# The first expert's weight loads without a wait, and the tile tables in two halves among the first units' low parts

## The chip, the cores and the metric

The kernel runs on one core of a Trainium2 chip. The metric is the device time of one execution in microseconds (us); lower is better. The times shown are medians of several executions.

## The reference, cut to what matters

Two transformer blocks over 2048 tokens of width 1024. The part around the change is the mixture of experts of the first block: every token goes to 4 of 32 experts, each with a gate-and-up product of 1024 x 2048, a clamped SwiGLU and a down product of 1024 x 1024.

```python
def moe(hn, router_w, router_b, w_gu, b_gu, w_down, b_down):
    ...
    top_vals, top_idx = lax.top_k(logits, TOP_K)
    gates = jax.nn.softmax(top_vals, axis=-1)
    flat_e = top_idx.reshape(-1)
    order = jnp.argsort(flat_e)
    sorted_e = flat_e[order]
    tok = order // TOP_K
    xs = xt[tok]
    group_sizes = jnp.bincount(flat_e, length=N_EXPERTS).astype(jnp.int32)
    gu = lax.ragged_dot(xs, w_gu, group_sizes) + b_gu[sorted_e]
    gate = jnp.minimum(gu[:, ::2], SWIGLU_LIMIT)
    up = jnp.clip(gu[:, 1::2], -SWIGLU_LIMIT, SWIGLU_LIMIT)
    act = (up + 1.0) * (gate * jax.nn.sigmoid(SWIGLU_ALPHA * gate))
    y = lax.ragged_dot(act.astype(w_down.dtype), w_down, group_sizes) + b_down[sorted_e]
    ...
```

## The kernel before

The kernel runs in phases, one after another with a barrier between them: a mixer phase with the router (it writes, for each expert, a list of its tokens to HBM, `tok_list`, and leaves on chip the order in which experts are taken, `order`, and a count per expert, `n_mid`), the expert phase, a combine phase, and the phases of the second block. The change lies in the first 50 us of the expert phase (`expert_phase`, from L981), which starts at about 963 us in the trace.

**Weights.** An expert's weights come in 25 units (`UNITS`): four chunks of 512 columns of the gate-and-up matrix, four units each (units 0 to 15), then nine for the down matrix. A unit of the usual size is 128 x 1024 words, 512 KB. SyncE (SP) loads a unit from HBM into one of five slots of `stage` (L1077), ScalarE (ACT) copies it to the rounded high part `w_hi` (`high`, L1151), and VectorE (DVE) subtracts to make the low part `w_lo` (`low`, L1282), which counts up `lo_done`. Load m waits until low part m-5 is made, since both use one slot. So the loads, high parts and low parts of a unit follow one another, five units in flight at most.

**Tokens.** For a tile of 128 tokens GpSimd (POOL) reads the token numbers from the list by two small DMAs (`ids`, L1106), and then gathers the rows by an indirect DMA (`rows`, L1112). TensorE (PE) transposes the rows (L1502). ACT makes the high part of the transposed tile and a bf16 copy (`x_high`, L1162 and L1164), DVE the low part (`x_low`, L1287). Only then can TensorE run the tile's products: for each chunk 16 products with the high weights (L968, L969) and 8 with the low ones (L971).

**What sets the order.** Each engine's instructions stand in an order written by hand, and an engine never takes a later one while it waits in an earlier one. At the start of the phase:

- SP reads the first expert's number, waits for the token numbers of the first tile (`ids_in`, line 1080), and then issues loads 0 to 4, and each later one as `lo_done` allows.
- ACT issues five DMAs for the biases (L1140, L1145), then `high` of units 0 and 1, then `x_high` of tile 0, then `high` of units 2 to 15. In the tile (`first`) follow `high` 16, 17, and so on.
- DVE makes the tile tables (`tables`, L1382 to L1409): `n_mid` sorted into the experts' order, and the running sums `starts` and `rows64`; then it signals `tables_ready`. Then `low` 0 and 1, `x_low`, `low` 2 to 13. In the tile follow `low` 14 to 16, and then `gates` of chunk 0 (L1306 to L1312), which adds the bias and frees the accumulator for chunk 3.
- PE transposes tile 0, then waits before chunk c of a new expert's first tile for `lo_done` of unit 4c+3, before chunk 0 also for `x_ready` (both parts of the tile), and before chunk 3 for `gates` of chunk 0, since chunk 3 uses the accumulator of chunk 0.
- All engines but SP wait for `tables_ready` after their part of tile 0, in `experts`, since the loop over the second and later tiles takes its bounds from the tables. POOL's part of tile 0 is its gather alone.

Of the kernel before, what the change touches and what calls it, by code (L numbers as in the profile page):

```python
# [8 lines left out]
F32 = mybir.dt.float32  # L9
I32 = mybir.dt.int32  # L10
U32 = mybir.dt.uint32
ALU = mybir.AluOpType
ACT = mybir.ActivationFunctionType
AX = mybir.AxisListType.X
# [24 lines left out]
E, TOPK, CAP = 32, 4, SEQ  # L39
# [912 lines left out]
GU_CHUNKS = 2 * FF // BANK  # L952
# [22 lines left out]
def gate_rows(w_lo):  # L975


    return w_lo[:, 0:GU_CHUNKS, :, :].rearrange("p c k n -> p (c k n)").bitcast(F32).rearrange("p (k n) -> p k n", n=D)


def expert_phase(nc, I, S):  # L981
# [6 lines left out]
    with ExitStack() as ctx:  # L988
# [5 lines left out]
        w_lo = S["w_lo_gate"]  # L994
# [9 lines left out]
        pre = sb("pre", [P, BANK])  # L1004
# [16 lines left out]
        s = {n: sem(n) for n in names}  # L1021
# [11 lines left out]
        def read(eng, table, i, most):  # L1033
            return eng.value_load(S[table][0:1, bass.ds(i, 1)], min_val=0, max_val=most)
# [27 lines left out]
        def place(m):  # L1062

            c, k0, k1 = UNITS[m]
            return c, slice(k0, k1), stage[:, m % STAGES, 0:k1 - k0, :]
# [5 lines left out]
        @block.sync  # L1071
        def _(sp):
            def load(m, e):
                c, ks, staged = place(m)
                name, col = ("expert_w_gate_up", c) if c < GU_CHUNKS else ("expert_w_down", c - GU_CHUNKS)
                w = I[name][0, bass.ds(e, 1), ks.start * P:ks.stop * P, col * BANK:(col + 1) * BANK].squeeze(0)
                sp.dma_start(staged, w.rearrange("(k p) n -> p k n", p=P)).then_inc(st_in[m % STAGES], 16)  # L1077

            e = read(sp, "order", 0, E - 1)
            sp.wait_ge(s["ids_in"], 32)  # L1080
            for m in range(N_UNITS):
                if m >= STAGES:
                    sp.wait_ge(s["lo_done"], m - STAGES + 1)
                load(m, e)
            with sp.Fori(1, E) as i:
                e = read(sp, "order", i, E - 1)
                for m in range(N_UNITS):
                    sp.wait_ge(s["lo_done"], i * N_UNITS + (m - STAGES + 1))
                    load(m, e)
            for k in range(KD):  # L1090
                if k % 2 == 0:
                    sp.wait_ge(s["low_free"], k // 2 + 1)
                sp.dma_start(gate_rows(S["w_lo_gate"])[:, k, :], I["ple_gate_w"][0, k * P:(k + 1) * P, :]).then_inc(S[f"gate_in{k}"], 16)
# [179 lines left out]
        def _(dve):  # L1273
# [4 lines left out]
            def low(e, m):  # L1278

                c, ks, staged = place(m)  # L1280
                dve.wait_ge(s["hi_done"], e * N_UNITS + (m + 1))
                dve.tensor_tensor(w_lo[:, c, ks, :], staged, w_hi[:, c, ks, :], ALU.subtract).then_inc(s["lo_done"], 1)  # L1282

            def x_low(g):

                dve.wait_ge(s["x_hi_ready"], g + 1)
                dve.tensor_tensor(x_lo[:, :, :], TX[:, :].rearrange("p (k c) -> p k c", c=P), x_hi[:, :, :],  # L1287
                                  ALU.subtract).then_inc(s["x_ready"], 1)
# [87 lines left out]
            row_of_e = lambda ap: ap.unsqueeze(1).to_broadcast([P, E, E])  # L1376
            row_of_i = lambda ap: ap.unsqueeze(2).to_broadcast([P, E, E])
            flat = stage[:, :, :, :].rearrange("p b k n -> p (b k n)")
            tc = Chain(dve, s["table_chain"])

            def numbers(iota, zero):
                tc.link(dve.memset(iota, 1.0))  # L1382
                tc.link(dve.memset(zero, 0.0))
                tc.link(dve.tensor_tensor_scan(iota, iota, zero, 0.0, ALU.add, ALU.add))
                tc.link(dve.tensor_scalar(iota, iota, -1.0, None, ALU.add))

            def tables():


                part = lambda n: w_lo[:, GU_CHUNKS + n // 2, n % 2 * 4:n % 2 * 4 + 4, :].bitcast(F32).rearrange("p k (i e) -> p (k i) e", e=E)  # L1390
                sel, picked = part(0), part(1)
                iota, zero, order, n_mid, sorted_mid, cnt_t, ends_t, cnt, ends = (pre[:, n * E:(n + 1) * E] for n in range(9))
                numbers(iota, zero)
                tc.link(dve.tensor_copy(order, S["order"][:, :]))
                tc.link(dve.tensor_copy(n_mid, S["n_mid"][:, :]))
                tc.link(dve.tensor_tensor(sel, row_of_e(iota), row_of_i(order), ALU.is_equal))
                tc.link(dve.tensor_tensor(picked, sel, row_of_e(n_mid), ALU.mult))
                tc.link(dve.tensor_reduce(sorted_mid, picked, AX, ALU.add))
                tc.link(dve.tensor_scalar(sorted_mid[:, 0:1], sorted_mid[:, 0:1], 1.0, None, ALU.max))
                tc.link(dve.tensor_scalar(sorted_mid[:, E - 1:E], sorted_mid[:, E - 1:E], 1.0, None, ALU.max))  # L1400
                dve.tensor_copy(S["n_mid"][:, :], sorted_mid)
                tc.link(dve.tensor_scalar(cnt_t, sorted_mid, 2.0, None, ALU.add))
                tc.link(dve.tensor_scalar(cnt, sorted_mid, 4.0, None, ALU.add))
                tc.link(dve.tensor_tensor_scan(ends_t, cnt_t, zero, 0.0, ALU.add, ALU.add))
                tc.link(dve.tensor_tensor_scan(ends, cnt, zero, 0.0, ALU.add, ALU.add))
                tc.link(dve.memset(S["starts"][:, 0:1], 0))
                tc.link(dve.memset(S["rows64"][:, 0:1], 0))
                tc.link(dve.tensor_copy(S["starts"][:, 1:E + 1], ends_t))
                tc.link(dve.tensor_copy(S["rows64"][:, 1:E + 1], ends))  # L1409
                dve.sem_inc(s["tables_ready"], 1)  # L1410

            sel, picked = (flat[:, n * E * E:(n + 1) * E * E].rearrange("p (i e) -> p i e", e=E) for n in range(2))
            which = flat[:, 2 * E * E:2 * E * E + TILES * TOPK * E].rearrange("p (n e) -> p n e", e=E)
            e_of, row_f = (flat[:, 4096 + n * TILES * TOPK:4096 + (n + 1) * TILES * TOPK] for n in range(2))
            to_row, iota, zero, order, begin = (flat[:, 4096 + (4 + n) * E:4096 + (5 + n) * E] for n in range(5))
# [26 lines left out]
            def last(e, g, n):  # L1442
# [42 lines left out]
                low(n, 13)  # L1485
                take_y(e, g)

            tables()
            for m in range(2):
                low(0, m)  # L1490
            x_low(0)
            for m in range(2, 14):
                low(0, m)
            experts(dve, first, mid, last)

# [1940 lines left out]
```

## Time and profile before

| what | value |
|---|---|
| median of 3 runs | 5496.25 us |
| lowest and highest of them | 5495.29 and 5498.11 us |
| the profiled execution: first to last instruction (its own time is not listed apart from that) | 5506.9 us |
| TensorE busy | 5150.5 us, 94% |
| VectorE busy | 3222.5 us, 59% |
| ScalarE busy | 2175.2 us, 39% |
| GpSimd busy | 628.4 us, 11% |
| expert phase, first DMA issue to the last gather issued | 964 to about 3486 us |

Times in the trace are microseconds from the first instruction. "Idle before" in a row of the timeline is how long that engine did nothing before the row, and the arrow names what ended the wait. Engines with a q at the end (SPq, ACTq) are the queue's side of an engine: what they did is issue a DMA. A row with "x5" merges five instructions of one kind, and its second number runs from the first's start to the last's end. PE is TensorE's matmul, PEld its weight load.

### The profile page before, as it was taken

The page shows a single profiled execution, that of the slowest core. Times are in us where ns is not written, and L with a number is a line of the kernel's source. Part 1 is how long each engine was busy: PE and PEld are TensorE (multiplying, and loading weights), DVE is VectorE, ACT ScalarE, POOL GpSimd, SP SyncE. Part 2 cuts the span into 40 slices and gives each one's busy share as a digit, 9 for nine tenths or more (in the row PEclk, how much of TensorE's full clock was granted, in tenths as well). Part 3 has the DMA queues.
Part 4 walks back from the last instruction along what each step waited for, and adds up shares of the span by engine and source line. Part 5 has one row for each costly group of instructions (what it writes and reads, how often), then busy time and mean ns, then how long its engine had stood idle before and what let it go on. Part 6 is the DMA issues. An engine that isn't in the chain of part 4 may idle for free. (4 is left out here: it accounts for less than half of the span.)

```text
span 5506.9 us, 77588 instructions
## 1 busy us (share of the span) xinstructions
PE 5150.5 (94%) x25057; PEld 3525.0 (64%) x25454; DVE 3222.5 (59%) x6024; ACT 2175.2 (39%) x3294; POOL 628.4 (11%) x862
## 2 busy tenths in 40 slices
PE   7999997799999999999999999699997699999698
PEld 4666664566666666666666666455555488888365
DVE  5444444667677677777777777543433644444266
ACT  4222221444444455555555555232223533333154
POOL 0000000000000000000000000010010199200000
PEclk9999998899999999999999999899998799999899
DMA  8777775655546467777777777432233300000533
GB/s 287 230 254 232 252 228 161 207 178 174 197 159 205 146 213 235 235 236 235 235 236 234 235 235 234 151 128 98 94 120 96 102 5 9 7 7 7 186 110 105
DMA packets 432865, 921.89 MB, mean 167 GB/s; under 512 B 62960, under 2 KB 87984, under 8 KB 432048
## 3 DMA queue, kind: packets, MB, share of 16 engines
q1 hardware_dynamic: 372208, 758.67, 42.1%
q10 hardware_dynamic: 33216, 87.05, 5.0%
q0 software_dynamic: 27280, 74.02, 4.2%
q8 instruction: 102, 1.67, 0.1%
q14 instruction: 59, 0.48, 0.0%
HBM read 774.11 MB, written 147.59 MB: 167 GB/s over the span
## 5 line engine op out<-in xcount | busy, mean ns | idle before, releaser
L1282 DVE TENSOR_TENSOR w_lo_gate<-stage,w_hi 128x1024 bf16<-128x1024 f32 (+1 forms) x800 | 929.8, 1179 | 195.3 <-ACT w_hi L1151 138.6
L1151 ACT ACTIVATE w_hi<-stage 128x1024 fp32r<-128x1024 f32 (+1 forms) x800 | 791.6, 1017 | 580.0 <-PE GU L971 295.1
L968 PE MATMUL GU<-w_hi,x_hl 128*128 128x512 f32 x2048 | 859.6, 420 | 18.7 <-DVE x_hl L1287 7.7
L969 PE MATMUL GU<-w_hi,x_hl 128*128 128x512 f32 x2048 | 811.3, 396 | 0.0
L971 PE MATMUL GU<-w_lo_gate,x_bf 128*128 128x512 bf16 x1920 | 481.4, 381 | 7.7
L968 PEld LDWEIGHTS GU<-w_hi,x_hl 128*128 128x128 f32 x2048 | 386.2, 189 | 134.7 <-issue 28.0
L968 PE MATMUL Y<-w_hi,a_hl 128*128 128x512 f32 x1024 | 456.7, 446 | 1.6 <-DVE a_hl L1293 1.6
L969 PEld LDWEIGHTS GU<-w_hi,x_hl 128*128 128x128 f32 x2048 | 387.3, 189 | 82.8
L969 PE MATMUL Y<-w_hi,a_hl 128*128 128x512 f32 x1024 | 404.4, 395 | 0.0
L971 PEld LDWEIGHTS GU<-w_lo_gate,x_bf 128*128 128x128 bf16 x2048 | 174.8, 98 | 255.5 <-issue 89.9
L2698 DVE TENSOR_REDUCE ntop<-SC 128x1 f32<-128x2048 f32 x64 | 146.7, 2292 | 267.6 <-PE SC L2806 267.6
L1157 ACT ACTIVATE acted<-pre 128x256 f32<-128x256 f32 (+1 forms) x304 | 131.9, 434 | 414.1 <-DVE pre L1310 404.0
L1112 POOL DMA_INDIRECT rows<-hn,ids x77 | 79.2, 1029 | 1776.7 <-PE TX L1502 1740.3
L971 PE MATMUL Y<-w_lo_gate,a_bf 128*128 128x512 bf16 x960 | 273.3, 383 | 4.4
L2831 PE MATMUL O<-shared 128*128 128x128 f32 x2048 | 265.0, 275 | 0.3 <-ACT shared L2611 0.3
L1306 DVE TENSOR_TENSOR pre<-GU,b_gu 128x512 f32<-128x512 f32 x256 | 175.6, 686 | 129.8 <-PE GU L971 129.2
L2831 PEld LDWEIGHTS O<-shared 128*128 128x128 f32 x2048 | 246.2, 191 | 1.8 <-ACT shared L2611 0.5
L810 PE MATMUL TR<-mixer_stage,c_all 128*128 128x512 f32 x512 | 230.8, 603 | 14.7 <-DMA mixer_stage<-w_out_rows 14.2
L968 PEld LDWEIGHTS Y<-w_hi,a_hl 128*128 128x128 f32 x1024 | 193.2, 189 | 53.1 <-DVE a_hl L1293 2.1
L1935 PE MATMUL G<-w_lo_gate,hT 128*128 128x512 f32 x512 | 225.2, 598 | 0.7 <-ACT hT L1726 0.7
L968 PE MATMUL Z<-w_in_hi,x_hi 128*128 128x512 f32 (+1 forms) x512 | 212.7, 415 | 3.2 <-ACT x_bf L1738 2.3
L969 PEld LDWEIGHTS Y<-w_hi,a_hl 128*128 128x128 f32 x1024 | 193.8, 189 | 33.7
(618 smaller groups left out, 9216.6 us busy)
## 6 DMA issues: line engine op xcount, KB each, us to landing
stage<-in_expert_w_gate_up_dram SPq DMA_DIRECT2D x512, 512.0 KB, 5.1
stage<-in_expert_w_down_dram SPq DMA_DIRECT2D x224, 512.0 KB, 6.6
mixer_stage<-w_in_lo SPq DMA_DIRECT2D x150, 512.0 KB
mixer_stage<-in_w_out_dram SPq DMA_DIRECT2D x65, 512.0 KB, 9.1
expert_rows<-zero_y SPq DMA_DIRECT2D x64, 512.0 KB, 6.5
mixer_stage<-w_out_rows SPq DMA_DIRECT2D x64, 512.0 KB
b_gu<-in_expert_b_gate_up_dram ACTq DMA_DIRECT2D x128, 256.0 KB, 4.7
expert_rows<-acted ACTq DMA_DIRECT2D x64, 512.0 KB, 3.3
```

Source lines behind the costliest of these rows:

```text
L810: mm = pe.matmul(out, catT[:, k, :], rows[:, q, :], start=(part == 0 and pair == 0 and q == 0), stop=(part == 1 and pair == 1 and q == 1))
L968: pe.matmul(out, high(k), w_high(k), start=(k == first), stop=False)
L969: pe.matmul(out, low(k), w_high(k), start=False, stop=False)
L971: mm = pe.matmul(out, short(k), w_low(k), start=False, stop=(k == last))
L1112: pool.indirect_dma_start(rows[:, :], None, S["hn"], bass.IndirectOffsetOnAxis(ap=ids[:, :], axis=0)).then_inc(s["rows_in"], 16)
L1151: act.activation(w_hi[:, c, ks, :], staged, ACT.Copy).then_inc(s["hi_done"], 1)
L1157: act.activation(act_of(c)[0:n], gate[0:n], ACT.Tanh, scale=ALPHA / 2).then_inc(s["tanh_ready"], 1)
L1282: dve.tensor_tensor(w_lo[:, c, ks, :], staged, w_hi[:, c, ks, :], ALU.subtract).then_inc(s["lo_done"], 1)
L1306: ch.link(dve.tensor_tensor(pre[:, :], GU[c][:, :], b_gu[:, cols], ALU.add))
L1935: mm = pe.matmul(G[:, n * BANK:(n + 1) * BANK], hT[:, k, :], w_gate[:, k, n * BANK:(n + 1) * BANK], start=(k == 0), stop=(k == KD - 1))
L2698: dve.tensor_reduce(ntop[:, h % 2:h % 2 + 1], SC[:, :], AX, ALU.min).then_inc(s["max_done"], 1)
L2831: mm = pe.matmul(O[:, h * P:(h + 1) * P], c_rows(kt), probsT[:, j, kt % 4 * P:(kt % 4 + 1) * P], start=(kt == 0), stop=(kt == TILES - 1))
```

## The change

SP no longer waits for the first tile's token numbers before it loads the first expert's weights. `tables` is cut in two, `sorted_counts` (up to the sorted `n_mid`) and `ends_of_tiles` (the running sums and `tables_ready`). DVE runs the first after `low` 0 to 2, then `low` 3 to 5, `x_low`, the second half, and `low` 6 to 13. Nothing else is changed, and nothing on ACT, PE or POOL.

```diff
             e = read(sp, "order", 0, E - 1)
-            sp.wait_ge(s["ids_in"], 32)
             for m in range(N_UNITS):
...
-            def tables():
...
+            def sorted_counts():
+
+                numbers(iota_t, zero_t)
+                tc.link(dve.tensor_copy(order_t, S["order"][:, :]))
                 tc.link(dve.tensor_copy(n_mid, S["n_mid"][:, :]))
...
                 dve.tensor_copy(S["n_mid"][:, :], sorted_mid)
+
+            def ends_of_tiles():
                 tc.link(dve.tensor_scalar(cnt_t, sorted_mid, 2.0, None, ALU.add))
                 tc.link(dve.tensor_scalar(cnt, sorted_mid, 4.0, None, ALU.add))
-                tc.link(dve.tensor_tensor_scan(ends_t, cnt_t, zero, 0.0, ALU.add, ALU.add))
-                tc.link(dve.tensor_tensor_scan(ends, cnt, zero, 0.0, ALU.add, ALU.add))
+                tc.link(dve.tensor_tensor_scan(ends_t, cnt_t, zero_t, 0.0, ALU.add, ALU.add))
+                tc.link(dve.tensor_tensor_scan(ends, cnt, zero_t, 0.0, ALU.add, ALU.add))
...
-            tables()
-            for m in range(2):
+            for m in range(3):
+                low(0, m)
+            sorted_counts()
+            for m in range(3, 6):
                 low(0, m)
             x_low(0)
-            for m in range(2, 14):
+            ends_of_tiles()
+            for m in range(6, 14):
                 low(0, m)
             experts(dve, first, mid, last)
```

On DVE, at the start of the expert phase, the order before is this (the first rows, L1382 to L1409, are the tables; L1282 is `low`, L1287 `x_low`, L1306 the first instruction of `gates`):

```order
1369 L1400 TENSOR_SCALAR pre<-pre 128x1 [waits table_chain]
1370 L1401 CAST n_mid<-pre 128x32 [waits table_chain]
1371 L1402 TENSOR_SCALAR pre<-pre 128x32
1377 L1408 CAST starts<-pre 128x32 [waits table_chain]
1378 L1409 CAST rows<-pre 128x32 [waits table_chain]
1379 L1282 TENSOR_TENSOR w_lo_gate<-stage,w_hi 128x1024 [waits table_chain,hi_done]
1380 L1282 TENSOR_TENSOR w_lo_gate<-stage,w_hi 128x1024 [waits hi_done]
1381 L1287 TENSOR_TENSOR x_hl<-TX,x_hl 128x8x128 [waits x_hi_ready]
1382 L1282 TENSOR_TENSOR w_lo_gate<-stage,w_hi 128x1024 [waits hi_done] x12
1385 L1282 TENSOR_TENSOR w_lo_gate<-stage,w_hi 128x1024 [waits hi_done] x3
1386 L1306 TENSOR_TENSOR pre<-GU,b_gu 128x512 [waits gu_ps,bg_in0]
```

With the change the same place of DVE's program reads as follows (its lines count one less up to the tables, so L1281 is `low`, L1286 `x_low`, and L1305 belongs to `gates`):

```order
1359 L1281 TENSOR_TENSOR w_lo_gate<-stage,w_hi 128x1024 [waits hi_done] x3
1360 L1381 MEMSET pre 128x32
1366 L1395 TENSOR_TENSOR w_lo_gate<-pre 128x1024 [waits table_chain]
1371 L1400 CAST n_mid<-pre 128x32 [waits table_chain]
1372 L1281 TENSOR_TENSOR w_lo_gate<-stage,w_hi 128x1024 [waits hi_done] x3
1373 L1286 TENSOR_TENSOR x_hl<-TX,x_hl 128x8x128 [waits x_hi_ready]
1374 L1403 TENSOR_SCALAR pre<-pre 128x32
1381 L1410 CAST rows<-pre 128x32 [waits table_chain]
1382 L1281 TENSOR_TENSOR w_lo_gate<-stage,w_hi 128x1024 [waits table_chain,hi_done]
1383 L1281 TENSOR_TENSOR w_lo_gate<-stage,w_hi 128x1024 [waits hi_done] x7
```

The twelve instructions up to the sorted `n_mid` moved from ahead of every low part to between `low` 2 and `low` 3, the other eight to between `x_low` and `low` 6; and `x_low` now stands behind `low` 5, where it stood behind `low` 1.

On SP, before the change, the first load carries the wait for the token numbers:

```order
315 L1034 TENSOR_LOAD order
316 L1034 ISA x2
317 L1077 ISA [waits ids_in]
318 L1077 DMA stage<-in_expert_w_gate_up_dram 128x2x512
319 L1077 ISA
```

In the changed kernel SP's place is this:

```order
315 L1034 TENSOR_LOAD order
316 L1034 ISA x2
317 L1077 ISA
318 L1077 DMA stage<-in_expert_w_gate_up_dram 128x2x512
319 L1077 ISA
```

The wait is gone and nothing has moved.

## Rows read from the trace of the kernel before

**Rows 1.** The page's part 1: busy us (share of the span) and count, by engine.

```profile
PE 5150.5 (94%) x25057; PEld 3525.0 (64%) x25454; DVE 3222.5 (59%) x6024; ACT 2175.2 (39%) x3294; POOL 628.4 (11%) x862
```

**Rows 2.** Windows: stretch, its length, each engine's busy us (count), clock, DMA share, GB/s.

```profile
947.00:987.00 40.00, 1.94 (x8) 1.57 (x8) 17.90 (x41) 6.99 (x8) 7.42 (x11) 0.50 0.43 145
1037.00:3470.00 2433.00, 2401.93 (x10972) 1612.86 (x11180) 1762.70 (x2686) 1210.10 (x1652) 153.80 (x221) 1.00 0.64 210
```

**Rows 3.** Timeline, TensorE: start, length, engine, line, operation, operands, [idle before <-what ended it].

```profile
980.11 1.94 PE L1502 MATMUL TX<-ident,rows 128*128 128x128 f32 x8 [33.63 <-DMA rows<-hn,ids]
987.60 0.80 PE L968 MATMUL GU<-w_hi,x_hl 128*128 128x512 f32 x1 [5.54 <-DVE w_lo_gate L1282]
...
995.41 0.58 PE L968 MATMUL GU<-w_hi,x_hl 128*128 128x512 f32 x1
...
1002.51 0.50 PE L968 MATMUL GU<-w_hi,x_hl 128*128 128x512 f32 x1 [1.28 <-DVE w_lo_gate L1282]
...
1012.45 0.47 PE L968 MATMUL GU<-w_hi,x_hl 128*128 128x512 f32 x1 [4.20 <-DVEq L1312]
...
1032.70 1.04 PE L1502 MATMUL TX<-ident,rows 128*128 128x128 f32 x8
```

**Rows 4.** Timeline, ScalarE, start of the expert phase.

```profile
964.38 3.60 ACTq L1140 DMA_DIRECT2D b_gu<-in_expert_b_gate_up_dram  x4
...
979.24 1.06 ACT L1151 ACTIVATE w_hi<-stage 128x1024 fp32r<-128x1024 f32 x1 [1.54 <-DMA stage<-in_expert_w_gate_up_dram]
982.09 1.02 ACT L1162 ACTIVATE x_hl<-TX 128x1024 fp32r<-128x1024 f32 x1 [1.79 <-PE TX L1502]
...
984.11 4.83 ACT L1151 ACTIVATE w_hi<-stage 128x1024 fp32r<-128x1024 f32 x5
```

**Rows 5.** Timeline, VectorE, start of the expert phase.

```profile
963.68 0.09 DVE L1382 MEMSET pre<- 128x32 f32 x1 [10.12 <-PEq L69]
...
969.11 0.17 DVE L1402 TENSOR_SCALAR pre<-pre 128x32 f32<-128x32 f32 x1
...
970.52 0.18 DVE L1409 CAST rows<-pre 128x32 int32<-128x32 f32 x1
...
983.14 1.22 DVE L1287 TENSOR_TENSOR x_hl<-TX,x_hl 128x1024 fp32r<-128x1024 f32 x1 [1.59 <-ACT x_hl L1162]
985.18 5.77 DVE L1282 TENSOR_TENSOR w_lo_gate<-stage,w_hi 128x1024 bf16<-128x1024 f32 x5 [0.81 <-ACT w_hi L1151]
...
1009.89 1.23 DVE L1282 TENSOR_TENSOR w_lo_gate<-stage,w_hi 128x1024 bf16<-128x1024 f32 x1 [0.78 <-ACT w_hi L1151]
1011.03 0.68 DVE L1306 TENSOR_TENSOR pre<-GU,b_gu 128x512 f32<-128x512 f32 x1
```

**Rows 6.** Timeline, SyncE's queue: the loads of the first expert's weights.

```profile
970.54 31.15 SPq L1077 DMA_DIRECT2D stage<-in_expert_w_gate_up_dram  x16
...
986.56 1.51 SPq L1077 DMA_DIRECT2D stage<-in_expert_w_gate_up_dram  x2
```

**Rows 7.** Timeline, GpSimd: token numbers and gathers of tiles 0 and 1.

```profile
965.95 1.15 POOL L1106 DMA_DIRECT2D ids<-tok_list  x2 [1.88 <-issue]
971.20 1.04 POOL L1112 DMA_INDIRECT rows<-hn,ids  x1 [4.10 <-DMA ids<-tok_list]
982.93 1.08 POOL L1106 DMA_DIRECT2D ids<-tok_list  x2 [10.69 <-issue]
987.76 1.81 POOL L1112 DMA_INDIRECT rows<-hn,ids  x1 [3.75 <-DMA ids<-tok_list]
```

**Rows 8.** Issue to landing: weight loads 960 to 1013 us; gather of tile 0; then all gathers.

```profile
DMA to landing us min/median/max: 4.6/6.2/9.5
...
rows<-hn,ids POOLq DMA_INDIRECT x1, 8.8
...
DMA to landing us min/median/max: 4.1/4.5/10.3
```

**Rows 9.** DMA queues, 976 to 980 us: packets, MB, share of 16 engines.

```profile
q1 hardware_dynamic: 517, 1.00, 66.5%
q0 software_dynamic: 138, 0.50, 34.7%
```

More of the change, by code:

```diff
@@ L1385, in numbers @@
                 tc.link(dve.tensor_scalar(iota, iota, -1.0, None, ALU.add))
-            def tables():
[L1390 to L1394, printed above, removed]
+            part = lambda n: w_lo[:, GU_CHUNKS + n // 2, n % 2 * 4:n % 2 * 4 + 4, :].bitcast(F32).rearrange("p k (i e) -> p (k i) e", e=E)
+            sel_t, picked_t = part(0), part(1)
+            iota_t, zero_t, order_t, n_mid, sorted_mid, cnt_t, ends_t, cnt, ends = (pre[:, n * E:(n + 1) * E] for n in range(9))
+            def sorted_counts():
+                numbers(iota_t, zero_t)
+                tc.link(dve.tensor_copy(order_t, S["order"][:, :]))
                 tc.link(dve.tensor_copy(n_mid, S["n_mid"][:, :]))
-                tc.link(dve.tensor_tensor(sel, row_of_e(iota), row_of_i(order), ALU.is_equal))
-                tc.link(dve.tensor_tensor(picked, sel, row_of_e(n_mid), ALU.mult))
-                tc.link(dve.tensor_reduce(sorted_mid, picked, AX, ALU.add))
+                tc.link(dve.tensor_tensor(sel_t, row_of_e(iota_t), row_of_i(order_t), ALU.is_equal))
+                tc.link(dve.tensor_tensor(picked_t, sel_t, row_of_e(n_mid), ALU.mult))
+                tc.link(dve.tensor_reduce(sorted_mid, picked_t, AX, ALU.add))
                 tc.link(dve.tensor_scalar(sorted_mid[:, 0:1], sorted_mid[:, 0:1], 1.0, None, ALU.max))
```

## The prediction

> **What bounds the kernel now.** I read the shares by engine first: TensorE is busy for 94% of the span [rows 1]. The windows then show which stretches differ. From 1037 to 3470 us, nearly all of the expert phase, TensorE is busy 2401.93 of 2433 us; what delays its start delays the end by the same amount. From 947 to 987 us it does 1.94 us of work in 40 us [rows 2]. So the change can only act on the phase's first 50 us, and what counts is when TensorE gets through them.
>
> The timelines of those 50 us give the chain. Until 980.11 TensorE waits for the gathered rows of tile 0 [rows 3]; call that moment S. ScalarE splits the transposed tile from 982.09, and since its program is in order, it takes up unit 2 only behind that, at 984.11 [rows 4]. VectorE makes low part 2 from 985.18 [rows 5]. Low part 3 ends at 987.60 and releases the first product. Chunks 1 and 2 start at 995.41 and 1002.51. Chunk 3 waits until 1012.45 for VectorE's `gates` of chunk 0 [rows 3], and that stands at 1011.03 behind low part 16, begun at 1009.89 [rows 5]. The last pacemaker is thus not TensorE but the ring load, high part, low part.
>
> The tables, 963.68 to 970.70, are on no path: VectorE ends with them and has nothing to do until unit 0 arrives [rows 5]. The loads' wait ends at 970.54 [rows 6]; without it the first load can be issued when ScalarE issues its first bias DMA after the same read of the order, 964.38 [rows 4]. That is 6.2 us earlier.
>
> **The change, part by part.**
>
> 1. *The earlier loads.* Only units 0 and 1 can use the 6.2 us. Unit 2's high part stands behind the tile's split, which waits for S. Loads 0 to 4 fill the five slots, low parts 0 and 1 release loads 5 and 6, and load 7 waits for low part 2, as it does now. Unit 2 is waiting in its slot at 984.11 already: no idle time stands before that row, which follows the split directly [rows 4]. Worth 0 by itself; it counts only through S (step 5).
>
> 2. *First half of the tables behind low part 2.* It takes 969.11 - 963.68 = 5.43 us [rows 5]. VectorE, idle after low part 1, cannot begin it, as low part 2 stands ahead and waits for the tile. With S unchanged, low part 2 ends at 985.18 + 1.23 = 986.4, and the half at 991.8. Five low parts take 5.77 us where one takes 1.23 [rows 5], a pitch of 1.14. So 3, 4 and 5 end at 995.3, and `x_low` (1.22, overlapping a little, as the low parts do) ends at about 996.4. TensorE needs it for the first product: 996.5 in place of 987.60, or 8.9 us later.
>
> 3. *Second half.* 969.11 to 970.70, 1.6 us: from 996.4 to 997.9, where `tables_ready` falls 27 us later than now. Low part 6 then ends at 999.1; now it ends at 985.18 + 5.77 = 990.95.
>
> 4. *The ring after that.* Loads 8 to 10 are issued behind low parts 3 to 5, from 993 on, so low parts 7 to 10 can follow at their pitch, and load 11 is issued behind low part 6. One turn from a low part to the one five later is: to the issue 0.15 (low part 2 ends 986.41, load 7 issued 986.56 [rows 6]), landing 6.2 (the median of this stretch [rows 8]), high part 1.06 [rows 4], low part 1.23 and 0.03 between them: 8.67. From 6 over 11 to 16 are two turns: 999.1 + 17.3 = 1016.4, and `gates` begins 0.1 earlier, 1016.3, in place of 1011.03: **+5.3 us**. With the shortest landing, 4.6, it is +2.1; with the longest, 9.5, +11.9 [rows 8]. TensorE's own work sets a floor: chunk 0 takes 995.41 - 987.60 = 7.8 us, chunk 1 without its idle time 1002.51 - 1.28 - 995.41 = 5.8, chunk 2 as much. So chunk 3 starts no earlier than 996.5 + 19.4 = 1015.9, against 1012.45: +3.5. I take +5.3. Of the 8.9 us some come back, as TensorE waits less for units 7 to 15. Behind chunk 3 the orders are unchanged, and the shift stays.
>
> 5. *S itself.* The token numbers now travel with weights beside them. Tile 0 took 5.25 us from their issue to the gather's, beside biases alone; tile 1 took 4.83, beside weights [rows 7]. Biases and weights together are in no row. The gather meets five loads in either kernel; it landed in 8.8 us, and gathers took from 4.1 to 10.3 with a median of 4.5 [rows 8]. From 976 to 980 us its queue got 0.50 MB while the weights' queue moved 1.00 MB [rows 9]: it gets its share beside loads. So S can fall by 4.3 (8.8 to 4.5) or rise by some 5.5 (numbers that need 10.3 where 4.83 was paid). One sign is against the change: the gather of tile 0 was issued in 1.04 us while VectorE idled, that of tile 1 in 1.81 while low parts ran, and it landed late [rows 7, 8]. With loads from 964.4, low part 0 falls at about 964.4 + 6.2 + 1.06 = 971.7, beside the first gather's issue at 971.20. I take the difference of these rows, **+0.8 us**.
> The Trainium skill (SBUF — State Buffer, Who interferes with whom) says that a VectorE instruction with two SBUF inputs, as a low part is, contends with a GpSimd instruction that reads SBUF; the two issue times agree, and by that rule alone the sum would be this same +0.8, without it 0.
> The Trainium skill (DMA: Bandwidth & Descriptors, Queues, rings and completion order) says that each DMA engine goes round the queues it has work for, packet by packet; rows 9 agree, and by it the token numbers would wait for two other queues in place of one, making S later.
>
> 6. *The second tile's gather.* GpSimd reads the tables before it: now `ids` goes out at 982.93, then only after 997.9, by the same 2.8 us (980.11 to 982.93) at about 1000.7. Plus 4.8 and 10.3 it is there by 1016, and TensorE wants it at 1032.70 [rows 3] and later: hidden. What it can cost is a slower load 16, inside the 9.5 of step 4.
>
> Sum: 5.3 + 0.8 = 6.1 us. The profiled execution spans 5506.9 us, 10.7 more than the median of the runs; with the change it would span 5513.0, and the median would be 5496.25 + 6.1 = **5502.3 us**. A measurement of this kernel can tell about 0.2%, 11 us, from no change. So I forecast a small loss that is within that.
>
> **The rivals.**
>
> *The gather comes early and pays for the tables.* If S is set mostly by loads that now are further along when the gather runs, S falls by up to 4.3: 5.3 - 4.3 = +1.0, 5497.3 us. For it: biases and first loads are spread over more time. Against it: loads 5 and 6 move up as well, so that as much is in flight.
>
> *Faster: the wait was the pacemaker.* If the stretch is set by the supply of weights, all moves up by 6.2 us: 5490.1. For it speaks TensorE's wait at 1002.51, which a low part ends whose unit came late [rows 3]. Against it, ScalarE's order holds unit 2 behind S however early the loads are. It decides only if unit 2 were late at 984.11, and it is not.
>
> *Slower by over 0.2%: the token numbers starve.* The wait kept two tiny DMAs ahead of 2.5 MB. If they land behind the weights, after 10.3 us in place of 4.8, S rises by 5.5 and the total is 5.3 + 5.5 + 0.8 = +11.6: 5507.9. The same follows if the two turns of the ring take 9.5 each, as beside a gather: +11.9 + 0.8, 5509. It decides once the gather is issued after about 976. For it: three queues at once is a load that no row shows. Against it: tile 1's numbers took 4.83 beside weights.
>
> *The change doesn't do what it says.* The order shows the wait gone, but the halves sit on VectorE's path rather than in its idle time; that is the forecast itself.
>
> **How the numbers follow.** Forecast (+3 to +9 us) 0.68, early gather 0.15, faster 0.05, starved 0.12. The range takes in the forecast with its bounds, the early gather and the lower part of the starved case: 5496.0 to 5508.5. Of the starved case about half is over 11 us; of the faster one little is beyond 11 us, which leaves faster 0.02, same 0.91, slower 0.07.
>
> **What would show it.** Right: first load issued at about 964.4; TensorE's transposes of tile 0 within 2 us of 980.9; the first half of the tables directly behind low part 2; the first product 16 to 17 us after the transposes start, where it is 7.5 now; chunk 3 at about 1018.5; from there on every row later by one constant. Wrong: transposes before 977 or after 984, a first product within 10 us of them, or low part 16 held by something other than load 16.

## The result, and the profile after

The changed kernel takes 5501.95 us (median of 20 runs), the kernel before, in the same comparison, 5494.51 us (20 runs): a ratio of 1.0014 with a 95% interval of 1.0008 to 1.0020, or about 7.4 us more. The range held. The interval lies above 1, so the loss is real, but it is under the 0.2% that the forecast called no change.

The profiled executions can't be compared by their spans: this one's is 5498.7 us, shorter than the one before, and most of that arises ahead of the change. The expert phase begins with GpSimd's first memset at 951.16 us after and at 963.40 before, although nothing before the phase was edited. So I count from that memset, and to TensorE's transposes of the second tile, from where TensorE has hardly a pause; this I call **the stretch**. Before, it runs from

```profile
963.40 0.21 POOL L122 MEMSET ident<- 128x128 f32 x1 [11.83 <-POOLq L69]
```

to 1032.70 [rows 3]: 69.3 us. After, GpSimd's and TensorE's timelines are these:

```profile
951.16 0.21 POOL L122 MEMSET ident<- 128x128 f32 x1 [10.87 <-POOLq L69]
...
953.72 1.15 POOL L1105 DMA_DIRECT2D ids<-tok_list  x2 [1.88 <-issue]
960.84 1.82 POOL L1111 DMA_INDIRECT rows<-hn,ids  x1 [5.98 <-DMA ids<-tok_list]
990.15 1.08 POOL L1105 DMA_DIRECT2D ids<-tok_list  x2 [27.49 <-issue]
998.36 2.02 POOL L1111 DMA_INDIRECT rows<-hn,ids  x1 [7.12 <-DMA ids<-tok_list]
```

```profile
969.42 1.94 PE L1506 MATMUL TX<-ident,rows 128*128 128x128 f32 x8 [34.22 <-DMA rows<-hn,ids]
985.82 0.77 PE L968 MATMUL GU<-w_hi,x_hl 128*128 128x512 f32 x1 [14.46 <-issue]
...
1006.64 0.47 PE L968 MATMUL GU<-w_hi,x_hl 128*128 128x512 f32 x1 [1.53 <-DVEq L1311]
...
1027.76 1.04 PE L1506 MATMUL TX<-ident,rows 128*128 128x128 f32 x8
```

The stretch is 1027.76 - 951.16 = 76.6 us, 7.3 more, about the measured loss. What lies behind it can be checked too: the next phase begins with the same memset, at 3530.62 before and 3525.32 after, so the expert phase took 2567.2 and 2574.2 us, 6.9 more. From the stretch's end to that memset it took 2496.8 to 2497.9 us in all fourteen profiles of this case: the stretch is passed on to the end of the phase within about 1 us. The phases behind it, which no edit touched, took 1976.3 before and 1973.4 after, and 1972.6 to 1977.0 over the fourteen: a difference of this size there says nothing of the change.

The stretch divides as follows (us; before from [rows 3]):

| part of the stretch | before | after | more |
|---|---|---|---|
| memset to first transposes (S) | 16.71 | 18.26 | 1.55 |
| (S to first product, part of the next) | 7.49 | 16.40 | 8.91 |
| S to chunk 3 | 32.34 | 37.22 | 4.88 |
| chunk 3 to second tile's transposes | 20.25 | 21.12 | 0.87 |

From here on, S stands for the time from the memset to the first transposes.

Where the first product waits is seen on VectorE and ScalarE; of VectorE's tables the first and last rows of each half are shown:

```profile
960.52 1.23 DVE L1281 TENSOR_TENSOR w_lo_gate<-stage,w_hi 128x1024 bf16<-128x1024 f32 x1 [0.38 <-ACT w_hi L1150]
974.49 1.23 DVE L1281 TENSOR_TENSOR w_lo_gate<-stage,w_hi 128x1024 bf16<-128x1024 f32 x1 [12.74 <-ACT w_hi L1150]
975.67 0.09 DVE L1381 MEMSET pre<- 128x32 f32 x1
...
981.00 0.18 DVE L1400 CAST n_mid<-pre 128x32 int32<-128x32 f32 x1
981.09 3.49 DVE L1281 TENSOR_TENSOR w_lo_gate<-stage,w_hi 128x1024 bf16<-128x1024 f32 x3
984.50 1.22 DVE L1286 TENSOR_TENSOR x_hl<-TX,x_hl 128x1024 fp32r<-128x1024 f32 x1
...
987.37 5.76 DVE L1281 TENSOR_TENSOR w_lo_gate<-stage,w_hi 128x1024 bf16<-128x1024 f32 x5
994.64 1.23 DVE L1281 TENSOR_TENSOR w_lo_gate<-stage,w_hi 128x1024 bf16<-128x1024 f32 x1 [1.51 <-ACT w_hi L1150]
...
1005.23 0.68 DVE L1305 TENSOR_TENSOR pre<-GU,b_gu 128x512 f32<-128x512 f32 x1
```

VectorE idles for 12.74 us, waiting for the high part of a unit that has long been in its slot (by 970 us the DMA engines have nothing left to do: busy for 0.04 of the window from 970 to 972), and then makes tables while TensorE waits. ScalarE tells why:

```profile
971.40 1.02 ACT L1161 ACTIVATE x_hl<-TX 128x1024 fp32r<-128x1024 f32 x1 [10.91 <-PE TX L1506]
...
973.42 4.83 ACT L1150 ACTIVATE w_hi<-stage 128x1024 fp32r<-128x1024 f32 x5
```

ScalarE waits 10.91 us for the tile, and takes the five units behind it without a pause.

### The profile page after: what moved, and what is told of

It is laid out like the page before. It is cut to its first block and busy times, and to the rows that moved or that the text cites. A ratio compares the mean times of both kernels' runs of the same rounds, so it can differ in the third digit from the quotient of the medians.

```text
span 5498.7 us, 77588 instructions
## 1 busy us (share of the span) xinstructions
PE 5145.0 (94%) x25057; PEld 3523.6 (64%) x25454; DVE 3220.8 (59%) x6024; ACT 2175.2 (40%) x3294; POOL 631.5 (11%) x862
## 5 line engine op out<-in xcount | busy, mean ns | idle before, releaser
L1281 DVE TENSOR_TENSOR w_lo_gate<-stage,w_hi 128x1024 bf16<-128x1024 f32 (+1 forms) x800 | 929.7, 1179 | 211.6 <-ACT w_hi L1150 155.0
L1305 DVE TENSOR_TENSOR pre<-GU,b_gu 128x512 f32<-128x512 f32 x256 | 175.7, 686 | 131.0 <-PE GU L971 130.2
```

The costliest lines, as they stand in the source:

```text
L1305: ch.link(dve.tensor_tensor(pre[:, :], GU[c][:, :], b_gu[:, cols], ALU.add))
```

## The experiments

Each runs against the kernel before on the same chip. A difference of a few us is near what these runs can tell (their intervals are 0.09% to either side, some 5 us), so the stretch of each profile is what I go by, with the medians beside it. The stretch itself differed by 0.7 us between two profiles of one kernel, so less than that is no difference either. The ratios are estimated together with their intervals and can differ from the quotient of the two medians by up to 0.0004. Where an edit touches ScalarE or VectorE at the start of the phase, the lines not shown are those of the kernel it starts from.

**The wait alone.** The kernel before without `sp.wait_ge(s["ids_in"], 32)`.

> SyncE's wait is removed, the tables stay whole and first on VectorE. The stretch is counted from GpSimd's first memset of the phase to TensorE's transposes of the second tile: 69.3 us before, 76.6 with the whole change. Theory (the wait's removal only delays the first gather): the first transposes stand 18.3 us after the memset (16.7 before), the first product 7.5 us behind them, the stretch is 70.9, the time +1.5 us. Rival (the earlier loads shorten the stretch once the tables are out of the way): stretch 63 to 67, time -3 to -6. Rival (the wait's removal is most of the loss): stretch 75 or more.

5504.01 us against 5502.79, ratio 1.0002 (0.9993 to 1.0011). Its timelines of GpSimd and of TensorE:

```profile
959.64 0.21 POOL L122 MEMSET ident<- 128x128 f32 x1 [11.03 <-POOLq L69]
...
969.33 1.04 POOL L1111 DMA_INDIRECT rows<-hn,ids  x1 [6.00 <-DMA ids<-tok_list]
```

```profile
976.58 1.94 PE L1501 MATMUL TX<-ident,rows 128*128 128x128 f32 x8 [33.06 <-DMA rows<-hn,ids]
984.06 0.80 PE L968 MATMUL GU<-w_hi,x_hl 128*128 128x512 f32 x1 [5.54 <-DVE w_lo_gate L1281]
...
1028.75 1.04 PE L1501 MATMUL TX<-ident,rows 128*128 128x128 f32 x8
```

The first product is 7.5 us behind the transposes, as said; the stretch is 69.1, as before. So both rivals fall, and my size too: the gather is issued 9.7 us after the memset (7.8 before), but lands sooner (in 7.1 us where it took 8.8), and the transposes stand 16.9 us after the memset, not 18.3.

**The split alone.** The changed kernel with the wait put back.

> VectorE's order is that of the change, but SyncE waits for the token numbers as before. Theory (the halves on VectorE's path are most of the loss): first transposes 16.7 us after the memset, first product 16.4 behind them, stretch 69.3 + 5.8 = 75.1, time +5.8 us. Rival (the halves cost only together with early loads, through traffic): stretch within 2 us of 69.3.

5505.53 us against 5502.79, ratio 1.0005 (0.9996 to 1.0014). Memset at 956.86, transposes at 973.94, then TensorE's timeline:

```profile
990.34 0.77 PE L968 MATMUL GU<-w_hi,x_hl 128*128 128x512 f32 x1 [14.46 <-issue]
...
1010.85 0.63 PE L968 MATMUL GU<-w_hi,x_hl 128*128 128x512 f32 x1 [2.22 <-DVEq L1312]
...
1031.34 1.04 PE L1507 MATMUL TX<-ident,rows 128*128 128x128 f32 x8
```

The stretch is 74.5, 5.2 more than before: most of the loss is the halves' place. The time by itself can't tell this from nothing.

**The tables in VectorE's idle time.** From the changed kernel:

```diff
-            for m in range(3):
+            for m in range(2):
                 low(0, m)
             sorted_counts()
-            for m in range(3, 6):
-                low(0, m)
-            x_low(0)
             ends_of_tiles()
-            for m in range(6, 14):
+            x_low(0)
+            for m in range(2, 14):
                 low(0, m)
```

> No wait; both halves of the tables stand together behind low part 1, and x_low comes back ahead of low part 2. VectorE is idle there for 12.7 us in the changed kernel, and the tables take 7. Theory (their place costs, not their work): hidden, as with the wait alone: first product 7.5 us behind the transposes, stretch 70.9, time +1.5 us. Rival (any table work behind a low part delays the phase, since GpSimd's second gather waits for it): stretch 73 or more.

5503.85 us against 5502.79, ratio 1.0005 (0.9996 to 1.0014). Transposes 17.2 us after the memset, first product 7.5 behind them, stretch 69.2: the same work costs nothing one low part earlier. What costs is that low part 2, which stands ahead of it in the change, can't be made before the tile is split. This edit also takes `x_low` back to its old place; what that place costs alone, the next run shows.

**Only x_low late.** The kernel before with `x_low` behind low part 5.

> The kernel before with one edit: x_low stands behind low part 5, as in the change, while the tables stay first and the wait stays. Theory (the ring of loads, high and low parts paces chunk 3, and a later first product is absorbed): first product about 11 us behind the first transposes (7.5 before), chunk 3 still about 32 behind them, stretch 69 to 70, time unchanged. Rival (the first product's delay passes through to the end): stretch 72.5 to 73.

5506.44 us against 5505.95, ratio 1.0002 (0.9993 to 1.0011). Transposes 16.5 us after the memset, first product 10.9 behind them, and chunk 3 33.5 behind them, where TensorE still waits 3.25 us; stretch 70.3, a little over the expected 69 to 70. Of 3.4 us by which the first product comes later, about 1 is left at the end: the ring paces chunk 3. By this estimate about 1 of the 5.2 us of the split alone is `x_low`'s place, and the other 4 are the tables'.

**Units before the split.** From the kernel before, without the wait; on ScalarE and VectorE:

```diff
-            for m in range(2):
+            for m in range(4):
                 high(0, m)
             x_high(0)
-            for m in range(2, 16):
+            for m in range(4, 16):
                 high(0, m)
...
             tables()
-            for m in range(2):
+            for m in range(4):
                 low(0, m)
             x_low(0)
-            for m in range(2, 14):
+            for m in range(4, 14):
                 low(0, m)
```

> No wait, tables whole and first; ScalarE makes high parts 0 to 3 ahead of x_high (0 and 1 before), VectorE low parts 0 to 3 ahead of x_low. Theory (unit 2 is held by the order behind the gather, not by its load): the early loads become usable: first product 4.5 us behind the first transposes (7.5 before), chunk 3 about 26 behind them (32.3 before); the transposes themselves 18.3 to 20 us after the memset, as loads 5 to 8 are now in flight with the gather; stretch 65 to 67, time -3 us. Rival (the supply of weights paces the stretch anyway): stretch as with the wait alone, 70 to 71.

5500.24 us against 5502.79, ratio 0.9995 (0.9986 to 1.0004). The memset is at 961.44, and TensorE's timeline reads:

```profile
978.70 1.94 PE L1501 MATMUL TX<-ident,rows 128*128 128x128 f32 x8 [33.55 <-DMA rows<-hn,ids]
983.05 0.77 PE L968 MATMUL GU<-w_hi,x_hl 128*128 128x512 f32 x1 [2.42 <-issue]
...
1027.34 1.04 PE L1501 MATMUL TX<-ident,rows 128*128 128x128 f32 x8
```

First product 4.4 us behind the transposes, stretch 65.9: it was the order that held the units back. Chunk 3 comes 28.4 us behind them, not the expected 26, and TensorE waits 3.88 us there: the ring still paces it.

**The same with the wait kept.**

> High and low parts 0 to 3 ahead of the tile's split, as in units_first, but with SyncE's wait kept. Theory (the order and the early loads are only worth something together): units 2 and 3 land 18 to 19.5 us after the memset, so the split stands behind them, first product at about 24 (24.2 before, 21.6 in units_first), stretch 68 to 69. Rival (the order alone brought the 3.4 us): stretch 65 to 66.

5498.58 us against 5502.68, ratio 0.9995 (0.9986 to 1.0004). Stretch 65.2: my theory falls, the rival holds. The order alone brought the gain. Units 2 and 3 do land late, as ScalarE's timeline shows:

```profile
976.66 1.06 ACT L1151 ACTIVATE w_hi<-stage 128x1024 fp32r<-128x1024 f32 x1 [2.00 <-DMA stage<-in_expert_w_gate_up_dram]
978.00 1.06 ACT L1151 ACTIVATE w_hi<-stage 128x1024 fp32r<-128x1024 f32 x1 [0.28 <-DMA stage<-in_expert_w_gate_up_dram]
978.96 1.00 ACT L1162 ACTIVATE x_hl<-TX 128x1024 fp32r<-128x1024 f32 x1
```

They are there 17.3 and 18.7 us after the memset (18 to 19.5 expected), and the split follows at 19.6; but the transposes, begun at 17.1, take 1.9 us themselves, so that the split is held back by only some 0.6 us. The first product comes 5.1 us behind the transposes, 0.8 later than without the wait, and nothing of that is left in the stretch. The removed wait is worth nothing measurable even to an order that could use it.

**The change once more.**

> The changed kernel unaltered, looked at once more, to see how far one profile's stretch can be trusted. Its first profile had the first transposes 18.3 us after the memset, while the three kernels without the wait since then had 16.9 to 17.3. Theory (the stretch is steady to about 1 us and the first gather's landing is what scatters): transposes 17 to 18.3 after the memset, first product 16.4 behind them, stretch 75.3 to 76.6. Rival (the wait's removal costs 1.5 us only together with the split): transposes at 18.3 again.

5509.26 us against 5502.68, ratio 1.0012 (1.0003 to 1.0021): the loss again. GpSimd's timeline, with TensorE's first transposes at 980.37:

```profile
961.98 0.21 POOL L122 MEMSET ident<- 128x128 f32 x1 [11.18 <-POOLq L69]
...
972.17 1.51 POOL L1111 DMA_INDIRECT rows<-hn,ids  x1 [6.50 <-DMA ids<-tok_list]
```

S is 18.4, as the rival said; the stretch is 75.9, within the theory's bounds, and the whole phase 5.9 us longer than before. Two profiles of the change have S at 18.3 and 18.4; the three kernels above without the wait have 16.9 to 17.3, so this part of the loss isn't scatter.

**Late biases in the change.** The five bias transfers are issued behind high part 6.

```diff
-            for c in range(GU_CHUNKS):
-                bias(0, c)
-            bias_down(0)
...
             x_high(0)
-            for m in range(2, 16):
+            for m in range(2, 7):
+                high(0, m)
+            for c in range(GU_CHUNKS):
+                bias(0, c)
+            bias_down(0)
+            for m in range(7, 16):
                 high(0, m)
```

> The changed kernel with the five bias transfers issued by ScalarE behind high part 6 in place of first of all. Theory (the token numbers came 1.9 us later because biases and weights were both in flight): the gather is issued about 7.5 us after the memset (9.7 in the changed kernel), the transposes and the stretch move up by 1 to 2 us: stretch 74 to 75. Rival (weights alone delay the token numbers as much): gather issued at 9.7, stretch 76 to 77.

5505.35 us against 5502.68, ratio 1.0004 (0.9995 to 1.0013). The gather is issued 9.4 us after the memset, so weights alone delay the token numbers nearly as much: the rival's first half. The gather then landed faster (6.9 us, transposes at 16.5), and the stretch is 74.2: inside the theory's bounds, but not for its reason.

The biases behind high part 6 in the kernel of *units before the split*:

> units_first with the biases behind high part 6. Theory (biases ahead of the token numbers hold the gather): gather issued at about 7.5 us, transposes about 15.3, stretch 63.5 to 65 (65.9 in units_first), time -5 us against the kernel before. Rival (bias issue on ScalarE in front of high part 7 gives it back): transposes at 15.3 but stretch 65.5 to 66.5.

5502.47 us against 5502.68, ratio 1.0000 (0.9991 to 1.0009). Gather issued at 10.0, transposes at 17.6, stretch 70.0. My numbers fall, for the gather as for the stretch, and the rival's stretch is passed too: TensorE waits 4.47 us for a low part before chunk 2. ScalarE issues transfers where high part 7 was due; it idles 1.71 us there, and the part begins some 2 us later than without the edit, counted from the memset. Units 9 and 10 then land late as well: ScalarE waits 2.41 and 4.29 us for them (1.62 and 3.57 without the edit).

**Wait kept, biases one by one.** From *the same with the wait kept*, with one bias transfer behind each of high parts 8 to 12.

> units_first_wait with the biases moved too: one bias transfer behind each of high parts 8 to 12. With the wait kept the token numbers travel alone. Theory (anything in flight beside them delays them): gather issued 6 to 6.8 us after the memset (7.6 in units_first_wait, 9.4 to 10.2 without the wait), first transposes at 15 to 16, stretch 63.5 to 64.5. Rival (3.3 us is their own latency): gather issued at 7.4 or later, stretch 65 or more.

5503.30 us against 5505.95, ratio 0.9999 (0.9990 to 1.0008). The DMA view of the first 12 us of the phase has the landing of the token numbers, in us:

```profile
ids<-tok_list POOLq DMA_DIRECT2D x2, 0.2 KB, 2.2
```

TensorE's timeline (memset at 959.38):

```profile
973.10 0.66 PE L1503 MATMUL TX<-ident,rows 128*128 128x128 f32 x2 [30.63 <-DMA rows<-hn,ids]
...
978.05 0.76 PE L968 MATMUL GU<-w_hi,x_hl 128*128 128x512 f32 x1 [3.01 <-issue]
...
1005.78 0.77 PE L968 MATMUL GU<-w_hi,x_hl 128*128 128x512 f32 x1 [7.89 <-DVEq L1313]
```

Alone, the numbers land in 2.2 us, and the gather is issued at 6.1: that half of the theory holds. But the 3.4 us are lost before chunk 3, where TensorE now waits 7.89 us: the stretch is 66.6. ScalarE's time for issuing the biases isn't what holds the ring: an issue takes 0.34 to 0.41 us, and from high part 7 to 16 each idle time of ScalarE (up to 3.00 us) ends with the landing of a unit. That the bias traffic is what slows these loads is likely, but wasn't tried apart.

**Gates early, and all three.** From *the same with the wait kept*; and once more together with the biases one by one.

```diff
                 dve.sem_inc(s["bf_zeroed"], 1)
+                if isinstance(g, int):
+                    gates(i, g, 0)
                 low(i, 14)
                 low(i, 15)
                 low(i, 16)
-                gates(i, g, 0)
+                if not isinstance(g, int):
+                    gates(i, g, 0)
```

> units_first_wait with gates of chunk 0 ahead of low part 14 for the first tile alone. Theory (chunk 3 waits for gates of chunk 0, which is ready long before but stands behind low part 16): TensorE's wait before chunk 3, 2.7 us there, goes nearly away, stretch 62.5 to 63.5 (65.2 there). Rival (low parts and gates share VectorE, so that the time comes back before the down product): stretch 64.5 to 65.5.

5503.70 us against 5505.95, ratio 0.9999 (0.9990 to 1.0008); stretch 66.0. The wait before chunk 3 shrinks from 2.67 to 0.59 us, and the wait before the first transposes of the activations grows from 3.47 to 5.49. These start 51.6 us after the memset, as against 51.4 without the edit: given back at once, on VectorE, as the rival had it (its 65.5 is passed by 0.5).

> Wait kept, units 0 to 3 ahead of the split, biases behind high parts 8 to 12, gates of chunk 0 early. Theory: the gains of the last two add: stretch 61 to 62.5, time -7 us against the kernel before, or a ratio of 0.9987. Rival (a bias now comes late for the early gates): stretch above 63.5.

5501.34 us against 5505.95, ratio **0.9990 (0.9981 to 0.9999)**; stretch 64.6. It misses the expected 61 to 62.5. By its stretch the rival holds, but not by its reason: `gates` of chunk 0 follows the low part ahead of it without a pause, so no bias is late for it; what TensorE waits for before chunk 3, 2.95 us, is a low part. It is the shortest stretch of all, though within 0.6 us of the order's alone, and the one version whose interval lies below 1 against the kernel before. Among twelve comparisons one such interval proves little by itself.

## Why the prediction was right

The time was forecast at +6.1 us, and came at +7.4. The two main parts of the sum, the halves on VectorE's path and the ring behind them, came as said; one term was too small and one is missing. That the median itself came within 0.4 us of the forecast 5502.3 is luck: the kernel before was 1.7 us faster in this comparison than in its three runs.

- *The earlier loads are worth nothing by themselves* (step 1): shown. Without the wait and with the old order the stretch is 69.1 against 69.3, and with an order that could use early units, 65.9 against 65.2 with the wait.
- *The first half behind low part 2* (step 2): the first product was forecast 16.4 us behind the transposes and came 16.40 behind them. The same tables one low part earlier cost nothing.
- *The ring* (step 4): chunk 3 was to move by 5.3 against S, and moved by 4.88 (3.7 in the second profile, near the floor of 3.5, with 0.68 us of waiting left). The recorded lower bound, +2.1 with the shortest landing, contradicts the step's own floor of 3.5. The two landings, taken as 6.2 each, were 4.8 and 7.0 in the first profile:

```profile
988.75 1.51 SPq L1077 DMA_DIRECT2D stage<-in_expert_w_gate_up_dram  x2
...
996.03 3.99 SPq L1077 DMA_DIRECT2D stage<-in_expert_w_down_dram  x2
```

```profile
993.55 1.06 ACT L1150 ACTIVATE w_hi<-stage 128x1024 fp32r<-128x1024 f32 x1 [2.18 <-DMA stage<-in_expert_w_gate_up_dram]
...
1002.99 1.06 ACT L1150 ACTIVATE w_hi<-stage 128x1024 fp32r<-128x1024 f32 x1 [0.27 <-DMA stage<-in_expert_w_down_dram]
```

  The first rows are SyncE's timeline, the issues of loads 11 and 16; the others ScalarE's, the high parts of these units. The second gather, which the tables held back to 998.36, shares the DMA engines with load 16, as step 6 had it.
- *S itself* (step 5) was mis-sized: +0.8 forecast, +1.55 and +1.7 measured. I read from tile 1 that weights don't delay the token numbers. They took 3.6 us to land before, 5.6 in the change, 5.3 with its biases moved away, and 2.2 with nothing beside them. The nearest row misled: in the three windows of 2 us from 982 us the DMA engines were busy for 0.83, 0.63 and 0.16, so tile 1's numbers travelled beside less and less. So the step's +0.8 is right in sign partly by luck: from the issue of the numbers to that of the gather 1.9 us more passed (7.12 in place of 5.25; 2.4 more in the second profile), which the sum put at nothing, and the gather's own landing went the other way, 8.8 to 8.4 (8.1 in the second), although its issue took longer.
- The gather's longer issue was forecast from one pair of rows, and it came: 1.82 us where it was 1.04. In the profile of the change low part 1 (960.52 to 961.75) is running when the gather is issued (960.84). In the wait-alone kernel it begins only after the gather has (969.77 against 969.33), and the issue takes 1.04. By the Trainium skill (SBUF — State Buffer, Who interferes with whom) such a low part contends with GpSimd's reading; the rows agree. S is a microsecond later in the change than in the other kernels without the wait; the longer issue, 0.78 and 0.47 us more, would be part of that, but no run isolated it, and the rest is open.
- *Not in the sum*: chunk 3 to the second tile, +0.87. The windows over the second half of chunk 3, before and then after, show it (columns as in [rows 2]; the third number from the end is TensorE's granted clock):

```profile
1018.90:1023.90 5.00, 4.99 (x16) 2.73 (x16) 4.79 (x9) 2.91 (x5) 0.00 (x0) 0.66 0.47 161
```

```profile
1013.10:1019.00 5.90, 5.90 (x16) 3.92 (x17) 5.68 (x9) 3.02 (x5) 0.00 (x0) 0.50 0.53 173
```

  The same 16 matmuls take 5.9 us in place of 5.0. The granted clock is 0.50, the lower of its two levels (1.2 and 2.4 GHz), over the whole window, behind a pause of 3.47 us; before, the pause was 1.86 and the clock 0.66 on average. The pause doesn't settle it alone: in *the same with the wait kept* it is 3.47 us too, but the clock rises within the window (0.72 on average) and the 16 matmuls are through in 5.04 us.
- *The signs*: the transposes of the first profile start at 969.42, which by the letter is a sign of being wrong ("before 977"). But the whole phase began 12.2 us earlier. Counted from the memset, the first load was to go out at 1.0 and did; the transposes were to start at 17.5 and started at 18.3 and 18.4; chunk 3 was to start at 55.1 and started at 55.5 and 54.4; and low part 16 was held by load 16. "Every row later by one constant" holds behind the second tile's transposes, not yet behind chunk 3.

## What to carry to other kernels

Before taking a wait away, find what the freed work meets next: here unit 2 and all behind it stood in ScalarE's order after its wait for the tile, so that the loads could start 6 us earlier and the first product not a moment sooner. Idle time on an in-order engine belongs to the instruction it waits in; work fits into it only if it stands ahead of that instruction, and one place later it is on the path. And a gain at the head of a ring of buffers has to be followed to the ring's last wait: moving the biases or the gates alone only moved TensorE's pause.

## What the runs showed of the hardware that I had not expected

Two DMAs of 64 words each took 2.2 us to land alone, 3.3 to 3.6 beside 1.5 MB of biases, 5.3 and 5.7 beside weight loads, and 5.6 to 6.0 beside both. The issue of the first tile's gather on GpSimd took 1.82 and 1.51 us in the two profiles of the change, where low part 1 was running as it began, and 1.04 us in the twelve profiles where none was. Two kernels with the same pause of 3.47 us on TensorE at the same place got its higher clock back at different times, one within the 5.0 us behind the pause, the other only after 5.9 us. And the start of the expert phase lay at 951 us in one profile and at 957 to 965 in the thirteen others, with the same program up to there: parts of a few us are better read from a fixed event than from spans.
